# Delta net, first direction: gates made among the norms, parts of convolutions and mixes on ScalarE, filling steps regrouped

## The reference

```python
qkv = silu(dwconv_centred(dn_qkv, dn_conv))          # centred convolution, 5 taps, 1536 channels
q = l2_normalize(q.reshape(bsz, seq, 4, 128)); k = l2_normalize(k...)
g = -exp(dn_a_log) * softplus(ab[:2] + dn_dt_bias);  beta = sigmoid(ab[2:])
o = gated_delta_chunked(q, k, v, g[0], beta[0]) + flip(gated_delta_chunked(flip(q), flip(k), flip(v), ...))
# in a chunk: decay = exp(G_i - G_j) below the diagonal, kk = (k*beta) k^T * decay,
#   T = strict(kk) + I, u = T^-1 (v*beta), w = T^-1 (k*beta*exp(G)), then the state of the chunks
s = x + mu[0]*(prev(x) - x) + mu[1]*(next(x) - x)    # token shift of the RWKV half, 1728 channels
```

## Time and profile before

| | us |
|---|---|
| median of 3 runs | 1874.29 (1871.32 to 1875.75) |
| the profiled execution | 1874.29 |
| its span, first to last instruction | 1873.0 |
| TensorE busy in the span | 1623.7 (87%) |
| VectorE busy | 1164.5 (62%) |
| ScalarE busy | 751.0 (40%) |
| TensorE's mean granted clock | 0.910 |

### The profile page before, as it was taken

One profiled execution on the slowest core, in us unless ns is written; L12 is line 12 of the kernel. 1 busy time (PEld: TensorE's weight loads), 2 busy tenths in 40 slices (PEclk: granted clock), 3 DMA queues, 4 the chain that ended last, 5 costly groups with the idle time before them and its releaser, 6 DMA issues.

```text
span 1873.0 us, 24185 instructions
## 1 busy us (share of the span) xinstructions
PE 1623.7 (87%) x10180; PEld 1434.7 (77%) x10180; DVE 1164.5 (62%) x1958; ACT 751.0 (40%) x1187; POOL 52.6 (3%) x50
## 2 busy tenths in 40 slices
PE   7988997999799889889998867856499888999877
PEld 6978886999699888779998766755389767885456
DVE  5577546555646665555556665555887757867555
ACT  4545434444435543444443432312122244645233
POOL 0000010000000001100000000010000000000000
PEclk9999998999899999989998787966697799999888
DMA  8543334555545333445556321000002065331042
GB/s 266 163 136 113 113 113 149 188 180 185 177 152 183 112 112 114 136 150 187 181 188 196 104 77 46 1 0 0 1 1 91 1 205 170 113 124 45 1 140 79
DMA packets 151178, 219.87 MB, mean 117 GB/s; under 512 B 6229, under 2 KB 110685, under 8 KB 150429
## 3 DMA queue, kind: packets, MB, share of 16 engines
q1 hardware_dynamic: 151068, 218.33, 36.4%
HBM read 217.25 MB, written 1.06 MB: 117 GB/s over the span
## 4 chain that ended last, share of the span: by engine, by line
PE 71%; DVE 18%; ACT 7%; DMA 3%; issue 1%; SPq 0%; DVEq 0%
PE bank L380 17%; PE bank L382 16%; PE bank L381 16%; PE bank L1895 4%; DVE weights_low L356 4%; PE bank L845 2%; PE bank L1986 2%; PE bank L3132 2%; ACT weights_high L343 2%; PE bank L2156 2%; PE bank L1952 1%; DVE place L2353 1%; PE bank L3158 1%; PE bank L458 1%; PE bank L2134 1%
## 5 line engine op out<-in xcount | busy, mean ns | idle before, releaser
L356 DVE TENSOR_TENSOR weights_low<-place,weights_high 128x1024 fp32r<-128x1024 f32 (+2 forms) x387 | 448.2, 1202 | 189.4 <-ACT weights_high L343 189.0
L343 ACT ACTIVATE weights_high<-place 128x1024 fp32r<-128x1024 f32 (+2 forms) x387 | 378.5, 1030 | 130.6 <-DMA place<-w_down_dram 44.0
L380 PE MATMUL bank<-hT_high,weights_high 128*128 128x256 f32 x1152 | 336.0, 292 | 5.7 <-DVE hT_low L477 4.1
L382 PE MATMUL bank<-hT_high,weights_low 128*128 128x256 f32 x1152 | 328.6, 285 | 0.0
L381 PE MATMUL bank<-hT_low,weights_high 128*128 128x256 f32 x1152 | 328.4, 285 | 0.0
L380 PEld LDWEIGHTS bank<-hT_high,weights_high 128*128 128x128 f32 x1152 | 221.3, 192 | 12.1 <-DVE hT_low L477 5.2
L381 PEld LDWEIGHTS bank<-hT_low,weights_high 128*128 128x128 f32 x1152 | 221.3, 192 | 0.6
L382 PEld LDWEIGHTS bank<-hT_high,weights_low 128*128 128x128 f32 x1152 | 220.9, 192 | 0.0
L1895 PE MATMUL bank<-place,place 128*128 128x128 f32 x624 | 91.3, 313 | 63.2 <-DVE place L2299 26.8
L1895 PEld LDWEIGHTS bank<-place,place 128*128 128x128 f32 x624 | 87.5, 225 | 68.0 <-issue 53.3
L382 PE MATMUL bank<-weights_high,branchT_low 128*128 128x512 f32 x256 | 101.0, 394 | 0.0
(11 more groups left out here) (413 smaller groups left out, 3368.0 us busy)
## 6 DMA issues: line engine op xcount, KB each, us to landing
place<-w_in_dram SPq DMA_DIRECT2D x48, 1024.0 KB, 5.3
place<-w_up_dram SPq DMA_DIRECT2D x32, 1024.0 KB, 5.4
place<-w_down_dram SPq DMA_DIRECT2D x32, 1024.0 KB, 5.1
place<-even_w_in_dram SPq DMA_DIRECT2D x17, 1024.0 KB, 5.2
place<-w_out_dram SPq DMA_DIRECT2D x16, 1024.0 KB, 5.2
place<-odd_w_in_dram SPq DMA_DIRECT2D x16, 1024.0 KB, 5.3
place<-w_branch_dram SPq DMA_DIRECT2D x12, 1024.0 KB, 5.0
place<-ple_gate_dram SPq DMA_DIRECT2D x8, 1024.0 KB, 5.2
```

The source lines that it names most:

```text
L343: nc.scalar.activation(high[:, lo:hi], self.raw[p % SLOTS][:, lo:hi], ACT.Copy).then_inc(*A("high", p, j))
L356: nc.vector.tensor_tensor(low[:, lo:hi], self.raw[p % SLOTS][:, lo:hi], high[:, lo:hi].bitcast(FP32), ALU.subtract).then_inc(*V())
L380: nc.tensor.matmul(out, left[0], right[0], start=first, stop=False)
L382: return nc.tensor.matmul(out, left[1], right[0], start=False, stop=last)
```

## The change

Four things, all in or before direction 0 of the delta net:

1. Convolutions: the middle tap (2) moves to ScalarE, as two scaled copies from the bank, issued behind the copy into `raw`; VectorE does taps 0, 1, 3 and 4 as multiply-adds on top. Shifted projections: the multiply by `mu_c` moves to ScalarE in the same way. Both banks are freed behind the scaled copies.
2. Norms of q and k: the squares move to ScalarE; those of q are made inside convolution group 5, those of k behind the norm of q.
3. Gates: ScalarE's Exp, Exp, Ln move from behind the transposes to between the two norms, waiting there for VectorE's `minus_abs`, which moves to behind the norm of q. VectorE's series moves from behind the transposes to right behind the norm of k.
4. Filling steps of direction 0: none in the two AT/NT/beta groups, three behind the compaction and before the rows (VectorE: before the substitution), five instead of four behind the rows; on VectorE these five stand behind the substitution and its transpose instead of before it. So two more are called before the levels, and all 29 are done in direction 0.

```diff
@@ delta_tensor
         four_tensor(k, ("beta", d, c), ...)
-        fill()
+        if d:
+            fill()
     inv = ("dn", d)
+    if d == 0:
+        fill(3)
     rows_tensor(k, e, e.inverse_dn, inv, d)
-    fill(4)
+    fill(4 if d else 5)
@@ shifted_vector
             V.wait_ge(("free", "shifted", n))
-            nc.vector.tensor_scalar(y, rr[:, 2:2 + S], e.mu_c[0:rows, f:f + 1], None, ALU.mult).then_inc(*V())
             for side, at in ((0, 1), (1, 3)):
-                V.wait_ge(V)
+                if side:
+                    V.wait_ge(V)
@@ l2_vector
-    V.wait_ge(*ready)
-    nc.vector.tensor_tensor(squares, y, y, ALU.mult).then_inc(*V("squares", *tag))
+    if squares is not None:
...
@@ even_vector
-            for tap in range(DN_CONV):
+            for tap in (0, 1, 3, 4):
+                V.wait_ge(V)
                 for j in range(2):
...
+                    nc.vector.scalar_tensor_tensor(y, r[:, j, tap:tap + S], e.cw[:, tap, f:f + 1], y, ALU.mult, ALU.add).then_inc(*V())
...
+    for _ in l2_vector(k, e, ("q",), e.qkvT[:, 0], None, table("ones")[:, 0:1], P ** -0.5):
         fill()
+    ea, z, ex = e.gate_columns()[:3]
+    nc.vector.scalar_tensor_tensor(ex, z, -1.0, z, ALU.mult, ALU.min).then_inc(*V("minus_abs"))
+    for _ in l2_vector(k, e, ("k",), e.qkvT[:, 1], None, table("ones")[:, 0:1], 1.0):
         fill()
+    delta_gates_vector(k, e)
     tokens_vector(k, ("k",), e.k_tok, fill)
     tokens_vector(k, ("v",), e.v_tok, fill)
-    delta_gates_vector(k, e)
@@ delta_vector
         nc.vector.tensor_tensor(NT[:, us], NT[:, us], split(k.bank("beta", d, c), 4, P), ALU.mult)...
-        fill()
+        if d:
+            fill()
...
     compact_vector(k, v, inv, NT, d, V)
-    fill(4)
+    fill(4 if d else 3)
     substitute_vector(k, v, inv, d)
+    if d == 0:
+        fill(5)
@@ shifted_scalar
+        part, m0, b = n // 2, 2 * (n % 2), split(k.bank("shifted", n), 2, S)
+        nc.scalar.activation(e.raw[n % 2][:, :, 2:2 + S], b, ACT.Copy).then_inc(*A())
+        if n == 0:
+            A.wait_ge(("mu_made",))
+        for j in range(2):
...
+            nc.scalar.activation(y, b[0:rows, j, :], ACT.Copy, scale=e.mu_c[0:rows, f:f + 1]
+                                 ).then_inc(*A(*(("free", "shifted", n) if j else ())))
@@ even_scalar
+            nc.scalar.activation(e.raw[m0 // 2][:, :, 2:2 + S], b, ACT.Copy).then_inc(*A())
+            if part + m0 == 0:
+                A.wait_ge(("even_loaded",))
+            for j in range(2):
+                f = 4 * part + m0 + j
+                nc.scalar.activation(e.qkvT[:, part, m0 + j, :], b[:, j, :], ACT.Copy, scale=e.cw[:, 2, f:f + 1]
+                                     ).then_inc(*A(*(("free", "conv", part, m0) if j else ())))
+            if (part, m0) == (2, 0):
+                A.wait_ge(A)
+                nc.scalar.activation(squares, e.qkvT[:, 0], ACT.Square).then_inc(*A("squares", "q"))
...
-    for _ in l2_scalar(k, e, ("k",), 1):
-        fill()
-    tokens_scalar(k, ("k",), e.k_tok, fill)
-    tokens_scalar(k, ("v",), e.v_tok, fill)
+    A.wait_ge(("l2", "q"))
+    nc.scalar.activation(squares, e.qkvT[:, 1], ACT.Square).then_inc(*A("squares", "k"))
     ea, z, ex, big, ser = e.gate_columns()
     nc.scalar.activation(ea, e.a_log, ACT.Exp).then_inc(*A("a_exp"))
     A.wait_ge(("minus_abs",))
     nc.scalar.activation(ex, ex, ACT.Exp).then_inc(*A())
     A.wait_ge(A)
     nc.scalar.activation(big, ex, ACT.Ln, bias=1.0).then_inc(*A("log_made"))
+    for _ in l2_scalar(k, e, ("k",), 1):
+        fill()
+    tokens_scalar(k, ("k",), e.k_tok, fill)
+    tokens_scalar(k, ("v",), e.v_tok, fill)
@@ delta_scalar
     fill(2)
-    fill()
-    fill()
+    fill(2 if d else 3)
     rows_scalar(k, e.inverse_dn, ("dn", d), d)
-    fill(4)
+    fill(4 if d else 5)
```

More of the change, by code:

```diff
@@ L2231, in l2_vector @@
     sums = e.stats[:, 88:88 + TT * 4 * n]
-    V.wait_ge(*ready)
-    nc.vector.tensor_tensor(squares, y, y, ALU.mult).then_inc(*V("squares", *tag))
+    if squares is not None:
+        V.wait_ge(*ready)
+        nc.vector.tensor_tensor(squares, y, y, ALU.mult).then_inc(*V("squares", *tag))
     yield
@@ L2357, in even_vector @@
     V.wait_ge(V)
-    nc.vector.tensor_scalar(e.mu_c, e.mu_c, -1.0, 1.0, ALU.mult, ALU.add).then_inc(*V())
+    nc.vector.tensor_scalar(e.mu_c, e.mu_c, -1.0, 1.0, ALU.mult, ALU.add).then_inc(*V("mu_made"))
     fill = Filler(silu_vector(k), shifted_vector(k, e), silu_vector(k, False))
@@ L2361, in even_vector @@
     delta_sums_vector(k, e)
-    squares = split(e.squares, 4, S)
-    for _ in l2_vector(k, e, ("q",), e.qkvT[:, 0], squares, table("ones")[:, 0:1], P ** -0.5, ("conv_silu", 0, 2)):
+    for _ in l2_vector(k, e, ("q",), e.qkvT[:, 0], None, table("ones")[:, 0:1], P ** -0.5):
         fill()
-    for _ in l2_vector(k, e, ("k",), e.qkvT[:, 1], squares, table("ones")[:, 0:1], 1.0, ("conv_silu", 1, 2), ("l2", "q")):
+    ea, z, ex = e.gate_columns()[:3]
+    nc.vector.scalar_tensor_tensor(ex, z, -1.0, z, ALU.mult, ALU.min).then_inc(*V("minus_abs"))
+    for _ in l2_vector(k, e, ("k",), e.qkvT[:, 1], None, table("ones")[:, 0:1], 1.0):
         fill()
+    delta_gates_vector(k, e)
     tokens_vector(k, ("k",), e.k_tok, fill)
     tokens_vector(k, ("v",), e.v_tok, fill)
-    delta_gates_vector(k, e)
     delta_vector(k, e, 0, fill)
@@ L2416, in delta_gates_vector @@
     ea, z, ex, big, ser = e.gate_columns()
-    nc.vector.scalar_tensor_tensor(ex, z, -1.0, z, ALU.mult, ALU.min).then_inc(*V("minus_abs"))
     V.wait_ge(("a_exp",))
@@ L2732, in shifted_scalar @@
         A.wait_ge(("shifted", n), ("shifted_done", n - 2) if n >= 2 else ("conv_done", 2, 2 * n))
-        nc.scalar.activation(e.raw[n % 2][:, :, 2:2 + S], split(k.bank("shifted", n), 2, S), ACT.Copy).then_inc(*A("free", "shifted", n))
+        part, m0, b = n // 2, 2 * (n % 2), split(k.bank("shifted", n), 2, S)
[3 more added lines that the diff above has]
+        for j in range(2):
+            rows, f = P if part < 3 or j == 0 else LORA, 4 * part + m0 + j
+            y = (e.rkvT[:, part, m0 + j, :] if part < 3 else e.loraT[:, j, :])[0:rows, :]
+            nc.scalar.activation(y, b[0:rows, j, :], ACT.Copy, scale=e.mu_c[0:rows, f:f + 1]
+                                 ).then_inc(*A(*(("free", "shifted", n) if j else ())))
         yield
@@ L2784, in even_scalar @@
     k.turn_scalar(("even_xT",), e.hT, KT)
+    squares = split(e.squares, 4, S)
     for part in range(3):
@@ L2788, in even_scalar @@
             A.wait_ge(("conv", part, m0), ("conv_done", part - 1, m0) if part else ("raw_zeroed", 0))
-            nc.scalar.activation(e.raw[m0 // 2][:, :, 2:2 + S], split(k.bank("conv", part, m0), 2, S), ACT.Copy
-                                 ).then_inc(*A("free", "conv", part, m0))
+            b = split(k.bank("conv", part, m0), 2, S)
+            nc.scalar.activation(e.raw[m0 // 2][:, :, 2:2 + S], b, ACT.Copy).then_inc(*A())
[8 more added lines that the diff above has]
+                nc.scalar.activation(squares, e.qkvT[:, 0], ACT.Square).then_inc(*A("squares", "q"))
             A.wait_ge(("conv_done", part, m0))
```

7 lines of the change are left out of this document (removed).

## The result

The changed kernel takes **1842.95 us** (median, 1839.58 to 1845.35), beside 1875.02 (1871.32 to 1876.28) for the kernel before in the same comparison: ratio 0.9823, 95% interval 0.9801 to 0.9846. A second comparison on another chip gave 1845.29 against 1874.05, 0.9844 (0.9826 to 0.9862). The forecast was 1846.3 with a range of 1838 to 1862.

A forecast was written before the change was run, and what follows sets the result against it. The prediction took chains hopping between engines, none full, to bound the stretch. Running totals ended at -27.9 on VectorE and -29 on ScalarE; taking -28 gave 1874.3 - 28 = 1846.3 us, range 1838 to 1862.

The forecast's parts named there:

- the solves: Behind the levels: TensorE's queue sets the time; no filling step left behind the last solve, some three us.
- steps 2 and 3: Filling steps on TensorE behind the q sums: same speeds as before, with rows of q applied 4.0 us earlier.
- up to 2 us more gained: Bound in the norms: extra gain if filling steps 2 and 3 run at 2.4 GHz from the start.
- Each idle stretch is followed by matmuls at half speed: Claim about TensorE's idle stretches in the convolutions and first direction: the granted clock has fallen to 0.50, 1.2 GHz.
- the wait costs 0.9: Between the norms, ScalarE waits at minus_abs for VectorE: 0.9 us given back, rows of k 3.1 us earlier.
- By the page this part would be 2.8 later: Norm of k: the skill page's 1.38 us drain per table load; as rival 1849 us, within ScalarE late, chance 0.06.
- Two mixings and two low parts, 8.65 us: VectorE's filling steps 16 to 20 between transpose and levels; TensorE and ScalarE need 5.64 us for the first product.
- 11.25 as before: The substitution, starting at 1111.9 us instead of 1140.4, takes an unchanged 11.25 us.
- low clock behind the 4.6 us, 0 to 4 us: Bound in the levels: cost of TensorE's low clock after waiting 4.6 us for VectorE, 0 to 4 us.
- more gain: Rival: low level ends earlier in the norms and hand-overs are short as written; 1834 to 1840 us, chance 0.10.
- TensorE at the low level more often: Rival: solves and AT/NT also start at 0.50; 7 to 15 us back, 1853 to 1862 us, chance 0.17.
- slower: Rival: TensorE's stage work stays at 1.2 GHz, one us more each; 52 us of it gives 1870 to 1890, chance 0.04.

The follow-up runs named there:

- u_squares: The changed kernel with the squares of q and k back on VectorE; 1850.90 us, ratio 0.9865 to the kernel before.
- sq_busy: The changed kernel with squares back on VectorE and fifteen unread products filling TensorE's stop before the sums of q; 1846.87 us, ratio 0.9843.
- u_steps: The changed kernel with the filling steps back in the AT/NT groups, as before the change; 1857.68 us, ratio 0.9903.
- spread: The changed kernel with VectorE's five steps dealt out: two behind the transpose, two between the levels, one behind the first right-hand side; 1837.87 us, ratio 0.9808.
- mask_early: The changed kernel with GpSimd's second-level mask of direction 0 made earlier, at the substitution's start, in its own buffer; 1840.90 us, ratio 0.9819.
- best: The kernel spread with the second level's mask also moved to the substitution's start; 1842.98 us, ratio 0.9834 to the kernel before.
- warm: The changed kernel with level 0's last group of products made four times over to keep TensorE busy; 1842.26 us, ratio 0.9835.
- only_steps: The kernel before with only the filling steps regrouped; 1863.13 us, ratio 0.9932.
- only_gates: The kernel before with only the gates moved among the norms; 1865.41 us, ratio 0.9951.
- u_gates: The changed kernel with the gates back behind the transposes; 1855.10 us, ratio 0.9891 to the kernel before.

## Right or wrong, step by step

Gain against the kernel before at each step, counted from the stage's start (the prediction's are its running totals):

| step | predicted | measured | this stretch alone: predicted, measured |
|---|---|---|---|
| convolutions | -1.8 | -1.5 | -1.8, -1.5 |
| rows of q applied | -4.0 | -8.1 | -2.2, -6.6 |
| rows of k applied | -3.1 | -6.4 | +0.9, +1.7 |
| first copy of sums | -7.9 | -11.5 | -4.8, -5.1 |
| exp(decay) done | -11.5 | -15.3 | -3.6, -3.8 |
| compaction done | -17.3 | -20.6 | -5.8, -5.3 |
| substitution starts | -28.5 | -32.2 | -11.2, -11.6 |
| second level done | -26.0 | -27.9 | +2.5, +4.3 |
| first copy, direction 1 | -27.9 | -31.5 | -1.9, -3.6 |

**Right**: the direction, the order of the parts, and five of nine stretches within 0.5 us. The convolution groups are 7.74 apart (7.7 said, 8.2 before). The q sums follow without idling. The gates stand between the rows of k and the token copy (1073.78 to 1076.2 in VectorE's timeline), and the cumulative sums at 1079.68 have no stop before them. The rows take 3.81 (3.9 said). TensorE is busy 90% of the stage ("over 85%"), and it is at the full level throughout the solves:

```profile
1135.00:1169.00 34.00, 32.19 (x213) 27.86 (x212) 13.23 (x21) 11.27 (x17) 0.00 (x0) 1.00 0.00 0
```

**Mis-sized, first: steps 2 and 3 "follow at the same speeds".** The bound beside it said "up to 2 us more gained" for 2.4 GHz. Measured: sums 1.84 instead of 3.27, steps 2 and 3 5.87 instead of 7.71, both by the clock, and step 1 done 1.6 earlier than forecast. That makes 4.9; 4.1 of it reach the rows of q, since VectorE was still at a low part there. It is as much as the whole excess of the stage (31.5 against 27.9). Of the 1.6 of step 1 some 0.5 is the clock, since its last products are at the full level; the rest is that it began 1.8 earlier in the stage than before, and not 0.95. The row that should have been followed up was the earlier trace rows: at 1048 to 1050 TensorE is at the low level in both kernels, and the question was when it rises. In the changed kernel it does so from 1050, while TensorE goes on working:

```profile
1048.00:1050.00 2.00, 2.00 (x6) 1.52 (x6) 1.67 (x6) 0.52 (x1) 0.00 (x0) 0.50 0.16 49
1050.00:1052.00 2.00, 2.00 (x17) 1.87 (x16) 0.91 (x1) 2.00 (x3) 0.00 (x0) 0.98 0.04 8
```

In the kernel before the rise came too, within half a microsecond of the end of step 1, but TensorE then stood, and just behind the stop of 3.44 us the level was down again:

```profile
1056.00:1058.00 2.00, 0.00 (x0) 0.00 (x0) 1.89 (x4) 1.99 (x5) 0.00 (x0) 1.00 0.00 0
1058.00:1060.00 2.00, 1.81 (x10) 1.81 (x11) 2.00 (x3) 1.85 (x2) 0.00 (x0) 0.64 0.03 8
```

I had put the clock into the rows (3.9 for 6.48) but not here: I took away a wait and kept the duration of what stood behind it. u_squares and sq_busy show that the stop has such a price.

One sentence of the prediction leans on the earlier trace rows wrongly: "Each idle stretch is followed by matmuls at half speed". No idle stretch stands ahead of those rows. In the kernel before TensorE was busy in all of every 2 us from 1036 to 1054, and the level went down amid that (0.72 from 1044 to 1046, 0.50 from there on), while it did products of 16 columns. The two rows above are the ones that bear the sentence out.

**Mis-sized, second: "the wait costs 0.9".** From the rows of q to those of k it cost 1.7 (12.04 us for 10.32). ScalarE stood at minus_abs for 0.29 only, and VectorE waited 5.15 for the high part behind three table loads:

```profile
1061.95 0.21 ACT L2827 ACTIVATE place<-place 128x16 f32<-128x16 f32 x1 [0.29 <-DVE place L2364]
1067.07 2.36 DVE L356 TENSOR_TENSOR weights_low<-place,weights_high 128x1024 fp32r<-128x1024 f32 x2 [5.15 <-ACT weights_high L343]
```

The chain itself took no longer than drawn: the scale was made 8.15 us after the rows of q, where the forecast had 8.6. But then the rows of k began 1.2 us late, since TensorE was still in step 5, at the low level behind a stop of 1.17:

```profile
1066.00:1072.00 6.00, 6.00 (x41) 6.00 (x40) 2.64 (x4) 3.47 (x5) 0.00 (x0) 0.72 0.24 82
```

The code of this part is the same in u_steps, spread, mask_early, best and warm, and but for the squares of k in sq_busy. In u_steps, spread, best, warm and sq_busy step 5 ran at the full level (spread: 1.00 from 1067.6 to 1073.6), the rows of k waited for the scale and not for TensorE, and the stretch took 10.99 in each: there the wait cost 0.7, about as forecast. In mask_early, and in the changed kernel profiled again, step 5 ran partly at the low level and the stretch took 12.03 and 12.04. So the 1.7 is 0.7 of wait and 1.05 of clock. Which executions have the second stays open: the stops before step 5 were 1.17, 0.85 and 1.39 us where the level was low (changed, the same again, mask_early), and 1.08, 0.87, 0.90 and 0.81 where it stayed full (u_steps, spread, best, warm).

"By the page this part would be 2.8 later": no drain shows at the table loads of the changed kernel. Each takes 1.28, it starts 0.01 to 0.03 behind the instruction before it in all but one of 38, and an instruction that doesn't wait for another engine starts within 0.02 of its end. That rival is out.

**Missing: GpSimd.** From the start of the substitution to the end of the levels the changed kernel gives back 4.3 instead of 2.5. "Two mixings and two low parts, 8.65 us" took 9.9: without the mask, which held one mixing for 1.8, they would have taken 8.1. In the kernel before that mask fell into VectorE's idling, so no row of before showed the price; the change filled the idling. The rest is two pieces. The second level took 4.4 instead of 3.65, with its products at 168 ns instead of 122, which lay within the bound "low clock behind the 4.6 us, 0 to 4 us". And the substitution with the transpose took 11.58, not "11.25 as before": it did so in every kernel with the regrouped steps (13.3 in the two with the early mask), for a reason that stays open.

**Too small: the solves**, 3.6 instead of 1.9. only_steps alone shows 4.2 there and u_steps loses 3.6, and only_gates, which keeps the two steps there, shows nothing (37.7 us, as before), so it goes with the two steps taken out of them; I had counted "some three us" for these and then let ScalarE's last Silu and load hide part of it.

**Whole time.** The median is 3.4 under the forecast, close to the stage's excess of 3.6. The profiled execution (1845.35) lies within 1 us of the forecast, and that is luck: the stage began 1.6 earlier and gained 3.6 more than forecast, and a rest 4.2 longer than before's took most of it back. Of the rivals, "more gain" had the right mechanism (the low level ends earlier in the norms) at about half its size. "TensorE at the low level more often" was right in two places only, step 5 and the levels. In "slower" the price doesn't follow its own rule: 52 us at the low level, at one more each, would give 1898 and not at most 1890. The parts undone one at a time cost 33.7 together, 2.2 more than all of them bring: they overlap little.

## What to carry to other kernels

A wait on TensorE has two prices: its length, and the low clock of what follows; take away the wait, and size the matmuls behind it anew at the other level. Where a change fills an engine's idling, look at what the other engines do in just that idling, GpSimd above all: an instruction of VectorE with two operands in SBUF stands still while a GpSimd instruction reads SBUF, so a mask that was free becomes 1.8 us on the path. And work queued ahead of a chain's next link (five filling steps before the levels) is best dealt out between the links, as spread did for 3.7 us (13.05 from X to the end of the levels, and 12.65 with the same order in best, against 16.75 and 16.62 in the two profiles of the changed kernel).

## What the runs showed of the hardware that I hadn't expected

- VectorE and GpSimd take turns instead of sharing: 0.20 became 1.97 us for a product of 24 elements, 1.88 became 3.66 for four multiply-adds, 2.35 became 4.17 for two low parts, each time about what was left of GpSimd's 2.0 us; and GpSimd's 2.0 became 3.05 behind VectorE. Reduces, and operations with an operand in a bank, went on.
- TensorE can be at 0.52 for 10 us in which it is busy for all 10 (1334 to 1344 above), in a place where another execution of nearly the same program has 1.00. The cause of these episodes was not looked for. Such episodes are part of why the time behind the stage lies between 667 and 675 us.
- The same stop of 2.4 us before level 0 was followed by full clock in three kernels (spread, warm, u_gates: 118 ns a product or less) and by a mix of both levels in the changed kernel, u_squares and sq_busy (150). Before step 5 a stop of 0.85 was followed by the low level and one of 0.90 by the full one.
